# Routed experts: which weight tiles are multiplied in plain fp32, and who prepares the tokens for them

## The reference

```
logits = (xt @ w_router).astype(float32)
top_vals, top_idx = lax.top_k(logits, 2)
combine = sum(one_hot(top_idx, 8) * softmax(top_vals)[..., None], axis=1)
for e in range(8):
    y = y + combine[:, e:e+1] * ((silu(xt @ w_gate[e]) * (xt @ w_up[e])) @ w_down[e])
```

## Time and profile before

| | us |
|---|---|
| median of 3 runs | 2561.56 |
| the profiled execution, its own time | 2561.27 |
| its span in the profile | 2559.5 |
| TensorE busy | 2411.1 |
| VectorE busy | 1958.3 |
| ScalarE busy | 1197.1 |
| GpSimd busy | 288.7 |

### The profile page before, as it was taken

One profiled execution on the slowest core, in us unless ns is written; L12 is line 12 of the kernel. 1 busy time (PEld: TensorE's weight loads), 2 busy tenths in 40 slices (PEclk: granted clock), 3 DMA queues, 4 the chain that ended last, 5 costly groups with the idle time before them and its releaser, 6 DMA issues.

```text
span 2559.5 us, 31541 instructions
## 1 busy us (share of the span) xinstructions
PE 2411.1 (94%) x12064; PEld 1872.2 (73%) x12064; DVE 1958.3 (77%) x3013; ACT 1197.1 (47%) x1271; POOL 288.7 (11%) x305
## 2 busy tenths in 40 slices
PE   9999999999999999999999999999999987878786
PEld 8899999899787788778778878888985543323332
DVE  5866754865888898888889888665668887787875
ACT  2564332273777777777777775317421111111111
POOL 0000000000000000000000000000013433333341
PEclk9999999999999999999999999999999999998899
DMA  8554654551999999999999996431779999999997
GB/s 247 157 190 132 198 182 144 156 165 52 420 366 398 416 406 375 421 414 380 400 416 399 370 415 203 133 99 61 236 261 415 421 421 422 421 421 422 421 421 294
DMA packets 238481, 786.64 MB, mean 307 GB/s; under 512 B 24368, under 2 KB 154544, under 8 KB 162288
## 3 DMA queue, kind: packets, MB, share of 16 engines
q1 hardware_dynamic: 198000, 504.46, 52.9%
q0 software_dynamic: 39184, 276.58, 26.5%
q10 hardware_dynamic: 1136, 3.43, 0.3%
HBM read 777.08 MB, written 7.34 MB: 306 GB/s over the span
## 4 chain that ended last, share of the span: by engine, by line
PE 69%; DMA 15%; DVE 10%; ACT 3%; issue 3%; POOL 0%; ACTq 0%; DVEq 0%; POOLq 0%
DMA dense_weights<-in_peer_rows,work 14%; PE banks L897 7%; PE banks L899 7%; PE banks L898 7%; PE banks L763 5%; PE banks L717 5%; PE banks L718 5%; PE banks L721 5%; PE banks L695 4%; PE banks L1380 4%; PE banks L1008 4%; PE banks L1009 4%; DVE weight_tiles_low L2643 2%; PE banks L1038 2%; PE banks L1022 2%
## 5 line engine op out<-in xcount | busy, mean ns | idle before, releaser
L1380 PE MATMUL banks<-dense_weights,work 128*128 128x512 f32 x888 | 422.1, 626 | 58.4 <-DVE work L3175 58.2
L2643 DVE TENSOR_TENSOR weight_tiles_low<-weight_tiles,weight_tiles_high 128x2048 fp32r<-128x2048 f32 x183 | 415.5, 2288 | 68.9 <-ACT weight_tiles_high L1919 68.3
L1380 PEld LDWEIGHTS banks<-dense_weights,work 128*128 128x128 f32 x888 | 174.9, 201 | 294.7 <-issue 203.7
L1919 ACT ACTIVATE weight_tiles_high<-weight_tiles 128x2048 fp32r<-128x2048 f32 x180 | 341.8, 1913 | 80.3 <-PE banks L899 74.9
L3165 DVE CUSTOM_DVE_ANT_0 dense_weights<-dense_weights,banks 128x1024 f32<-128x1024 f32 x222 | 266.6, 1218 | 68.6 <-DMA dense_weights<-in_peer_rows,work 67.5
L2269 DVE TENSOR_TENSOR weight_tiles_low<-weight_tiles,weight_tiles_high 128x2048 fp32r<-128x2048 f32 x93 | 212.2, 2289 | 130.7 <-ACT weight_tiles_high L1681 130.5
L2183 ACT ACTIVATE work<-work,small 128x2 f32<-128x2 f32 x129 | 38.1, 295 | 539.5 <-DVE work L3165 539.0
L1657 POOL DMA_INDIRECT dense_weights<-in_peer_rows,work x222 | 209.2, 942 | 595.4 <-DVE work L3121 315.1
L1681 ACT ACTIVATE weight_tiles_high<-weight_tiles 128x2048 fp32r<-128x2048 f32 x93 | 177.2, 1909 | 57.3 <-PE banks L899 31.2
L717 PE MATMUL banks<-weight_tiles_high 128*128 128x256 f32 x800 | 188.9, 281 | 5.0 <-issue 3.1
L718 PE MATMUL banks<-weight_tiles_high,weight_tiles_low 128*128 128x256 f32 x800 | 187.4, 279 | 0.0
(11 more groups left out here) (547 smaller groups left out, 5064.6 us busy)
## 6 DMA issues: line engine op xcount, KB each, us to landing
weight_tiles<-in_moe_tiles SPq DMA_DIRECT2D x196, 1024.0 KB, 10.9
dense_weights<-in_moe_tiles SPq DMA_DIRECT2D x84, 1024.0 KB, 11.2
weight_tiles<-in_w_in SPq DMA_DIRECT2D x38, 1024.0 KB, 5.5
spare_row<-in_moe_tiles SPq DMA_DIRECT2D x28, 1024.0 KB, 11.4
work<-in_moe_tiles SPq DMA_DIRECT2D x28, 1024.0 KB, 11.9
weight_tiles<-in_w_xkv SPq DMA_DIRECT2D x16, 1024.0 KB, 5.4
weight_tiles<-in_ffn_w_gate SPq DMA_DIRECT2D x11, 1024.0 KB, 5.3
weight_tiles<-in_ffn_w_up SPq DMA_DIRECT2D x11, 1024.0 KB, 5.4
```

The lines of the kernel that those rows point to most:

```text
L1380: mm = pe.matmul(halves[half], diag[(first + j) % 8], pair_row(first + j)[:, 1, half * 512:(half + 1) * 512], start=False, stop=end and j ...
L1919: act.activation(high_tile(par, j), raw_tile(par, j), ACT.Copy).then_inc(g.high, 1)
L2643: dve.tensor_tensor(low_tile(par, j), raw_tile(par, j), high_tile(par, j).bitcast(F32), ALU.subtract).then_inc(g.split, 1)
```

## The change

`SMALL_PLAIN` becomes empty and `LARGE_PLAIN` is (5, 12, 19, 26): four gate and up tiles of each large turn are multiplied in plain fp32, every tile of a small turn is split. In a large turn the tokens' high and low parts lie in separate tiles, so a plain product needs their sum: a new tile `xe_sum` (128 x 1024 fp32, in a free part of the work buffer). GpSimd adds the two parts for it, once before the first large turn and once in each small turn but the last, behind its gather and ahead of the adding of output rows. TensorE waits for the sum before it uses a plain tile of a large turn. The numbering of split tiles follows the new lists, and two semaphores of the start of the program (ones ready, constants ready) are made one, to make room for the new one.

```diff
-SMALL_PLAIN = (3, 11, 19, 27, 33, 39)
+LARGE_PLAIN, SMALL_PLAIN = (5, 12, 19, 26), ()
...
+        groups.plain = (LARGE_PLAIN, SMALL_PLAIN) if name == "experts" else ((), ())
+        groups.summed = sem(f"{name}_tokens_summed") if name == "experts" else None
...
+        xe_sum = view(3328, KT, P)
...
-            pe.wait_ge(ones_ready, 1)
+            pe.wait_ge(consts_ready, 1)
...
-                                if is_plain(small, j):
+                                if j in g.plain[par]:
                                     raw = plain(j, KT // 2)
+                                    if not small:
+                                        pe.wait_ge(g.summed, p + 1)
+                                    tokens = xe_high.bitcast(F32) if small else xe_sum
...
-                                        mm = pe.matmul(bank, xe_high[:, k, :].bitcast(F32), raw[:, i, :], start=(k == 0), stop=(k == KT - 1))
+                                        mm = pe.matmul(bank, tokens[:, k, :], raw[:, i, :], start=(k == 0), stop=(k == KT - 1))
...
             g = passes[0]
+
+            def sum_tokens():
+                pool.tensor_tensor(xe_sum, xe_high.bitcast(F32), xe_low.bitcast(F32), ALU.add).then_inc(g.summed, 1)
+
+            pool.wait_ge(g.took_sems["v"], g.took["first", 4])
+            sum_tokens()
             for e in range(N_EXP):
...
+                if kind:
+                    pool.wait_ge(g.took_sems["v"], g.took["s_gather", KT // 2 - 1] + e * g.takes["v"])
+                    sum_tokens()
                 pool.wait_ge(g.took_sems["a"], g.took[kind + "down", 1] + e * g.takes["a"])
```

More of the change, by code:

```diff
@@ L195, in __init__ @@
         groups.raw_loads, groups.loaded_before = raw_loads, 0 if name == "experts" else 16 * N_EXP * EXP_TILES // RAW_SLOTS
-        groups.plain_in_pair = 0 if name != "experts" else len(SMALL_PLAIN)
+        groups.plain = (LARGE_PLAIN, SMALL_PLAIN) if name == "experts" else ((), ())
+        groups.summed = sem(f"{name}_tokens_summed") if name == "experts" else None
         groups.used, groups.marks = [], EXP_MARKS
@@ L374, in high_tile @@
             return high_tiles[:, (par * EXP_TILES + j) % HIGH_SLOTS, :]
-        def is_plain(small, j):
-            return small and j in SMALL_PLAIN
         def split_number(g, p, par, j):
-            before = [i for i in range(j) if not is_plain(par == 1 and g.plain_in_pair > 0, i)]
-            return p * (2 * EXP_TILES - g.plain_in_pair) + par * EXP_TILES + len(before) + 1
+            split = [[i for i in range(EXP_TILES) if i not in plain] for plain in g.plain]
+            return p * (len(split[0]) + len(split[1])) + par * len(split[0]) + sum(i < j for i in split[par]) + 1
         def loaded_number(g, p, par, j):
@@ L512, in two_blocks @@
         params_loaded = sem("params_loaded")
-        ones_ready, consts_ready = sem("ones_ready"), sem("consts_ready")
+        consts_ready = sem("ones_and_constants_ready")
         sq_ready = sem("squares_ready")
@@ L743, in _ @@
             G.end(mm)
-            pe.wait_ge(consts_ready, 1)
+            pe.wait_ge(consts_ready, 2)
             norm_sums(("mix_ms", 0))
@@ L1057, in turn @@
                             halves.append(g.begin("a", (down_, 1)))
-                        if is_plain(small, GATE_UP + d):
+                        if GATE_UP + d in g.plain[par]:
                             raw = plain(GATE_UP + d, 2)
@@ L1588, in _ @@
             step = Steps(pool, pool_step)
-            pool.memset(ones[:, :], 1.0).then_inc(ones_ready, 1)
+            pool.memset(ones[:, :], 1.0).then_inc(consts_ready, 1)
             step.then(pool.memset(ident[:, :], 0.0))
@@ L1914, in round_tile @@
                         p, par, j = p + par, 1 - par, j - EXP_TILES
-                    if is_plain(n == 0 and par == 1, j):
+                    if j in g.plain[par]:
                         return
```

## The result

The changed kernel takes 2587.93 us (median of 4 runs, 2586.31 to 2592.10) against 2559.62 us before (4 runs, 2557.22 to 2565.13). The ratio is 1.0106 with a 95% interval of 1.0094 to 1.0118: about 1% slower, where no change was forecast (2565 us, range 2555 to 2578).

What follows compares the result with a forecast made beforehand. TensorE was taken to bound both kinds of turn, with the change making VectorE the small turn's bound. Four pairs of +2.9 - 2.1 gave +3 us: 2565 us, called no change, range 2555 to 2578.

Steps and rivals of the forecast that it cites:

- A plain tile: Large turn, TensorE: four more plain tiles at 0.72 us each add 2.9 us, giving 122.6 us.
- a cycle of 9.65 us in a chunk: Small turn, VectorE: four low parts, two shorter pieces of 0.34 us and a 0.17 us stall make 9.65 us.
- their allowance: Small turn, weight loads: 14.3 us to landing where 19 are allowed; the queue grows 2 to 3 us and stays inside.
- The step that failed first: End of small turn: 2.2 us from TensorE's last product to the next turn's first, within a turn of 102.5 us.
- The sign that I had given for a wrong forecast: Small turns staying at 104.6 us or above, or falling below 99, would show the forecast wrong.
- The second: GpSimd's addition beside VectorE's low parts: slows VectorE between 0 and 2 us, four times; taken as 0.
- rival (a): Small turns, step 31 to 36: GpSimd's addition shuts VectorE out, 4 x 2 to 2.3 us, 2573 us; chance 0.24.
- My argument against it: GpSimd's descriptor work beside low parts shows nothing on VectorE, so the addition's effect there was taken as 0.
- The third: Small turn: with VectorE as bound it takes 102.5 us, a gain of 2.1 us.
- the trade of tiles: All four pairs: +2.9 us in each large turn against -2.1 in each small one, +3 us in all.
- (b): Small turns: engines trip each other, 0.5 to 0.7 us a chunk, or loads lag; 2573 to 2578 us; chance 0.18.
- (c): Small turns near TensorE's 94.8 us, 2534 us in all; weak form 98.9, 2550 us; chance 0.11 in weak form.

Runs made afterwards that it cites:

- the kernel with both losses out: Changed kernel with TensorE's hardware loop written out and without GpSimd's addition: 2558.96 us, ratio 0.9987 to the kernel before.
- the last experiment: Changed kernel with hardware loop kept, no addition, plain tiles 21, 36 and 41 in small turns, none in large ones: 2543.56 us, ratio 0.9944 to the kernel before.
- the large half alone: Changed kernel with addition and large turns' four plain tiles, but the six plain tiles of small turns kept: 2584.44 us, ratio 1.0089 to the kernel before.

## Why the prediction was wrong

**Right, with its size.** A plain tile costs 0.72 us more than a split one in a large turn: 122.5 measured for 122.6, wherever the clock was full. The small turn changes its bound to VectorE, with a cycle of 9.65 us in a chunk: the multiplies of the changed kernel start at 1037.62, 1047.28 and 1056.94, 9.66 apart. Without addition and loop, small turns are 101.4 to 101.9 where I had 102.5 with 2.2 us of gap in it, so 100.3; I was short by a bit over 1 us. The loads stayed inside their allowance: medians up to 16.2 us to landing in the changed kernel's small turn, with 19 allowed.

**The step that failed first** is in the small turn: "from its last product to the first one of the next turn there are 2.2 us". I took this gap of the earlier trace rows over as a constant. It was the visible part of 6.7 us that run from VectorE's last low part of the turn to the first product behind the branch; the other part was covered only because TensorE was late at that place. In a turn that VectorE bounds, TensorE uses that low part as soon as it is there, and 4.9 us are seen. To this comes what I had not in the sum at all, the half clock after a gap of that length: large turns after the first fell from 124.6 to 122.5 on average with the loop written out. Against my sum the two are 3 x (4.9 - 2.2) + 3 x 2.1 = 14 us, less the 1.7 of half clock that the kernel before had already; against the same kernel without its loop 3 x (4.9 - 0.5) + 3 x 2.1 = 20, as measured. I had asked of the row labelled "issue" what it was worth, and not what started it. The sign that I had given for a wrong forecast, small turns of 104.6 us or above, came true with 107.9.

**The second** is GpSimd's addition, where I took 0 of a range of 0 to 2 us each time: 2.2 us on VectorE in each small turn, 3.7 to 5.1 in the first large turn (2.1, and the half clock behind the longer wait). That is 10 to 12 us by the turns and 8 to 9 by the medians. This was rival (a), at 0.24, with a price of 8 to 9 us; the mechanism was right, but the half clock in the first large turn was not in its price. With the 3.5 us of the trade below, these make up the 25 us between forecast and result.

The rule of the Trainium skill that rival (a) was set beside (SBUF — State Buffer, "Who interferes with whom": a VectorE instruction with two SBUF inputs and a GpSimd one that reads SBUF exclude each other, and the later waits) holds here: 8.91 us for three low parts in place of 6.69. The estimate of 2.2 us from GPSIMD Engine Reference, section 3.1, is near the 2.44 measured. My argument against it, that indirect DMAs beside low parts do no harm, was about another kind of work. One part of (a) was wrong: it is not needed that VectorE be the bound of the turn. With 15 us of slack in the turn the addition cost as much, since at that step VectorE's lead was gone, and 20 to 22 us into a large turn, where VectorE waits for roundings, it cost nothing.

**The third** is a term of the wrong size, what the small turn gains. With neither loop nor addition in either kernel it is 1.3, 0.8, 1.3 and 1.7 us for the 2.1 forecast, against 2.9 lost in each large turn. So the trade of tiles costs 6.5 us and not 3. That the kernel with both losses out took 2559 us, near the forecast, is luck: the loop that was written out in it gave back what the kernel before still paid.

**The first two together** made the range too narrow: each rival was priced by itself, and the range held one of them. Rivals (b) and (c) did not happen.

**Still open:** what TensorE does in the 6.7 us. They are gone when the branch is gone, and work queued behind the last wait doesn't shorten them. A 16 KB transfer of instructions stands in each of them, 2.7 to 2.8 us before the end, and not where the loop is written out; that speaks for a fetch of the loop's first instructions, but no run changed the fetch alone, and the 3.7 to 4.1 us ahead of it have no cause shown. Nor is it settled what starts the time. VectorE's next low part, the first one behind the branch and the one that the profile names, follows 2.2 us after in all 21 turn ends, so a chain of 4.3 to 4.7 us from there fits as well, the last experiment included.

## What to carry to other kernels

A gap at a loop's branch can be the visible end of a chain of fixed length, here 6.7 us from another engine's last release, and a faster or better balanced body can uncover it: measure from that release and not from the engine's own last instruction, and either write the loop out or put long work that waits for nothing late as the body's last. Work moved to an idle engine costs what it shuts out on its neighbour at that very spot; look at the lead there, not at the idle time of the whole stage. When moving work makes another engine the bound of a stage, move only until the two sums meet (here two or three plain tiles in a small turn, not six or none), and compare the price of a tile in each stage where it could go. And compare kernels that have the same losses: beside the kernel before with its loop, a costly trade looked even.

## What the runs showed of the hardware

- From VectorE's last low part of a turn to the first product after TensorE's hardware loop: 6.6 to 7.0 us in 18 turn ends of six kernels, and 6.8 to 6.9 in the seventh after another tile. The profile named VectorE as the releaser in the changed kernel, though its low part had been ready for 4.5 us.
- In the same 21 turn ends a 16 KB transfer of the instruction queue began 2.7 to 2.8 us before that first product.
- A gap of 4.2 to 5.1 us on TensorE was followed by the lower clock for 3.4 to 6.8 us in each of the 12 large turns behind it, a gap of 2.1 to 2.5 us in one of six (before, and the large half alone), a gap of 1.7 or 1.8 us in none of three.
- GpSimd's addition held up VectorE's small instructions with one SBUF input as well: a cast of 128 x 8 took 2.30 us in place of 0.17.
